# Prompt attention values taken head by head, with the high and low parts of values and of probabilities side by side

## What is computed

```python
    logits = jnp.einsum('bthd,btkhd->bhtk', q, k_sel).astype(jnp.float32) * (HEAD_DIM ** -0.5)
    logits = jnp.where(valid[:, None], logits, NEG)
    p = jax.nn.softmax(logits, axis=-1).astype(v_sel.dtype)
    return jnp.einsum('bhtk,btkhd->bthd', p, v_sel)
```

## Time and profile before

| what | value |
|---|---|
| median of 3 runs | 2734.62 us (2734.62 to 2734.95) |
| span of the profiled execution, first to last instruction | 2732.7 us |
| PE busy | 2707.3 us (99%), 18804 matmuls |
| DVE busy | 1729.2 us (63%) |
| ACT busy | 1103.5 us (40%) |
| POOL busy | 999.8 us (37%) |
| granted TensorE clock | 0.998 |

### The profile page before, as it was taken

How to read it: one execution, slowest core, us unless ns; L and a number is a source line. 1 busy time by engine, 2 the same in 40 slices (tenths; PEclk the granted TensorE clock), 3 DMA queues, 4 the chain that set the end, 5 groups by cost and what they waited for, 6 DMA issues and landing times. The chain is left out here.

```text
span 2732.7 us, 46951 instructions
## 1 busy us (share of the span) xinstructions
PE 2707.3 (99%) x18804; PEld 2646.4 (97%) x18804; DVE 1729.2 (63%) x2801; ACT 1103.5 (40%) x1858; POOL 999.8 (37%) x610
## 2 busy tenths in 40 slices
PE   9999999999999999999999999999999999999998
PEld 8999999998999999999999999999989999999997
DVE  8747576887433693838685647668773347837475
ACT  5324244636322352424443333454463224424242
POOL 2333333345433333333333333333544333333332
PEclk9999999999999999999999999999999999999999
DMA  3222222233122222222222222222332222222222
GB/s 118 99 71 93 77 87 93 88 124 125 63 71 91 75 73 84 78 93 78 94 77 85 70 95 78 92 86 88 132 109 70 77 88 74 75 79 78 93 78 85
DMA packets 72853, 238.04 MB, mean 87 GB/s; under 512 B 8304, under 2 KB 17264, under 8 KB 72176
## 3 DMA queue, kind: packets, MB, share of 16 engines
q1 hardware_dynamic: 57888, 208.30, 22.1%
q10 hardware_dynamic: 14800, 27.51, 2.9%
HBM read 227.52 MB, written 8.27 MB: 86 GB/s over the span
## 5 line engine op out<-in xcount | busy, mean ns | idle before, releaser
L498 POOL TENSOR_TENSOR w_lo<-w_raw,w_hi 128x1024 fp32r<-128x1024 f32 (+1 forms) x254 | 600.0, 2365 | 962.8 <-ACT w_hi L1131 947.7
L1131 ACT ACTIVATE w_hi<-w_raw 128x1024 fp32r<-128x1024 f32 (+1 forms) x238 | 250.2, 1051 | 796.1 <-PE lin L635 660.8
L635 PE MATMUL lin<-h_hi,w_hi 128*128 128x320 f32 x1600 | 373.8, 315 | 2.9 <-DVE tmp L1614 2.7
L635 PE MATMUL lin<-h_hi,w_lo 128*128 128x320 f32 x1600 | 364.6, 309 | 0.0
L635 PE MATMUL lin<-h_lo,w_hi 128*128 128x320 f32 x1600 | 364.1, 309 | 0.0
L635 PE MATMUL lin<-g_hi,w_lo 128*128 128x320 f32 x1408 | 320.9, 309 | 0.0
L635 PE MATMUL lin<-g_lo,w_hi 128*128 128x320 f32 x1408 | 320.8, 309 | 0.0
L635 PE MATMUL lin<-g_hi,w_hi 128*128 128x320 f32 x1408 | 320.7, 309 | 0.0
L550 POOL TENSOR_TENSOR lo_A<-raw_even,hi_A 128x512 fp32r<-128x512 f32 x120 | 167.8, 1398 | 376.3 <-ACT hi_A L1185 376.3
L635 PEld LDWEIGHTS lin<-h_hi,w_hi 128*128 128x128 f32 x1600 | 265.2, 188 | 15.9 <-issue 11.3
L635 PEld LDWEIGHTS lin<-h_lo,w_hi 128*128 128x128 f32 x1600 | 267.5, 188 | 0.0
(11 more groups left out here) (334 smaller groups left out, 6215.6 us busy)
## 6 DMA issues: line engine op xcount, KB each, us to landing
w_raw<-wts SPq DMA_DIRECT2D x240, 512.0 KB, 3.5
raw_even<-wts SPq DMA_DIRECT2D x88, 512.0 KB, 4.4
raw_odd<-wts SPq DMA_DIRECT2D x64, 512.0 KB, 4.2
caches<-kcache_in ACTq DMA_DIRECT2D x16, 512.0 KB, 4.0
caches<-vcache_in ACTq DMA_DIRECT2D x16, 512.0 KB, 4.7
x<-x_in SPq DMA_DIRECT2D x8, 320.0 KB, 6.6
k_out<-kT ACTq DMA_DIRECT2D x2, 1280.0 KB, 4.6
v_out<-v_sb ACTq DMA_DIRECT2D x2, 1280.0 KB, 8.6
```

The lines of the kernel that those rows point to most:

```text
L498: ins = nc.gpsimd.tensor_tensor(w_lo[:, s, cols], w_raw[:, s, cols], w_hi[:, s, cols].bitcast(F), ALU.subtract)
L635: ins = nc.tensor.matmul(out[:, half, :], w, a[:, half * HALF:(half + 1) * HALF], start=first and n == 0, stop=last and n == 2)
L1131: nc.scalar.activation(w_hi[:, s, 0:cols], w_raw[:, s, 0:cols], ACT.Copy).then_inc(hi_ready.sem, 1)
```

## The change

The weight block of the value product now holds one head: 64 columns of high and 64 columns of low values, side by side (hi, lo for head 0; lo, hi for head 1, so that the high rows land on the same 64 partitions as before). The moving operand is 256 columns of one head's probabilities: 128 high, 128 low. One pass of nb matmuls per head gives all four products, in 256 columns of PSUM of its own. ScalarE copies the lo x hi block across to the other 64 partitions (`keep_cross`, new, at step u+4 before `take_turned`), and VectorE adds hi x hi, hi x lo and lo x hi in four `tensor_tensor` instructions in place of two copies. The values' parts get buffers of their own, and splitting them takes two instructions of half the size on ScalarE and on VectorE. Before the last `conv_hi` ScalarE now waits for the last value product.

```diff
@@ weigh (PE)
-                    for i in range(3):
-                        if i == 2:
+                    for par in range(2):
+                        if par == 0:
+                            pe.wait_ge(pT_split.sem, pT_split.count(L, PROMPT_BEFORE[u]))
+                        else:
                             pe.wait_ge(pT_split.sem, pT_split.count(L, PROMPT_BEFORE[u] + 1))
                         for b in range(nb):
-                            v = v_lo[:, b, pair * P:(pair + 1) * P] if i == 0 else v_hi[pair % 2][:, b, :]
-                            ins = nc.tensor.matmul(out[:, 0:2 * P], v,
-                                                   pT[a][:, b, i // 2, :, :].rearrange("p two q -> p (two q)"),
-                                                   start=b == i == 0, stop=b == nb - 1 and i == 2)
+                            v = v_parts[pair % 2][b // 2][:, b % 2, 2 * par:2 * par + 2, :]
+                            ins = nc.tensor.matmul(out[:, par * 2 * P:(par + 1) * 2 * P],
+                                                   v.rearrange("p two d -> p (two d)"),
+                                                   pT[a][:, b, par, :, :].rearrange("p two q -> p (two q)"),
+                                                   start=b == 0, stop=b == nb - 1)
                 ins.then_inc(pv_done.sem, 1)
@@ split_v and keep_cross (ACT)
-                nc.scalar.activation(v_hi[pair % 2][:, :, :], v_sb[:, 0:4, pair * P:(pair + 1) * P],
-                                     ACT.Copy).then_inc(v_hi_done.sem, 1)
+                for half in range(2):
+                    ins = nc.scalar.activation(v_parts[pair % 2][half][:, :, 0:4:3, :], v_blocks(pair, half), ACT.Copy)
+                ins.then_inc(v_hi_done.sem, 1)
+
+            def keep_cross(L, u):
+
+                _, a, h = ATT_UNITS[u]
+                k = PROMPT_BEFORE[u] // 2
+                act.wait_ge(pv_done.sem, pv_done.count(L, ITEM_OF[u] + 1))
+                if k >= 2:
+                    act.wait_ge(o_halved.sem, o_halved.count(L, k - 1))
+                for par in range(2):
+                    to, from_ = slice(64 * par, 64 * par + 64), slice(64 - 64 * par, 128 - 64 * par)
+                    ins = nc.scalar.activation(cross[to, k % 2, :],
+                                               out_banks[ITEM_OF[u] % 2][from_, par * 2 * P:par * 2 * P + P], ACT.Copy)
+                ins.then_inc(cross_kept.sem, 1)
@@ the step loop (ACT), ahead of take_turned(L, step - 2)
+                    if 0 <= step - 4 < NU and ATT_UNITS[step - 4][0] == "prompt" and step - 4 == ITEMS[ITEM_OF[step - 4]][-1]:
+                        keep_cross(L, step - 4)
@@ behind the loop (ACT)
                 split(L, GATE_AT + 2)
+                act.wait_ge(pv_done.sem, pv_done.count(L, NI))
                 conv_hi(CB - 1)
@@ keep_out (DVE)
-                    dve.wait_ge(pv_done.sem, pv_done.count(L, ITEM_OF[u] + 1))
+                    k = PROMPT_BEFORE[u] // 2
+                    dve.wait_ge(cross_kept.sem, cross_kept.count(L, k + 1))
                     for par, lane in enumerate(lanes):
-                        ins = nc.vector.tensor_copy(qT[lane, h // 2, a * P:(a + 1) * P],
-                                                    out[lane, par * P:(par + 1) * P])
+                        ins = nc.vector.tensor_tensor(qT[lane, h // 2, a * P:(a + 1) * P], cross[lane, k % 2, :],
+                                                      out[lane, par * 2 * P:par * 2 * P + P], ALU.add)
+                    ins.then_inc(o_halved.sem, 1)
+                    dve.wait_ge(o_halved.sem, o_halved.count(L, k + 1))
+                    for par, lane in enumerate(lanes):
+                        o = qT[lane, h // 2, a * P:(a + 1) * P]
+                        ins = nc.vector.tensor_tensor(o, o, out[lane, par * 2 * P + P:(par + 1) * 2 * P], ALU.add)
                 ins.then_inc(o_kept.sem, 1)
@@ lo_v (DVE)
-                nc.vector.tensor_tensor(v_lo[:, 0:4, cols], v_sb[:, 0:4, cols], v_hi[pair % 2][:, :, :].bitcast(F),
-                                        ALU.subtract).then_inc(v_split.sem, 1)
+                for half in range(2):
+                    parts_ = v_parts[pair % 2][half]
+                    ins = nc.vector.tensor_tensor(parts_[:, :, 1:3, :], v_blocks(pair, half),
+                                                  parts_[:, :, 0:4:3, :].bitcast(F), ALU.subtract)
+                ins.then_inc(v_split.sem, 1)
```

More of the change, by code:

```diff
@@ L169, in build @@
         k_lo = at("k_lo", [P, AB, T], R, mix_at + 4 * part)
-        v_lo = at("v_lo", [P, TT, ATT_W], R, mix_at + 11 * part)
-        v_hi = [at(f"v_hi{i}", [P, 4, P], R, mix_at + 8 * part + 2048 * i) for i in range(2)]
+        v_parts = [[at(f"v_parts{i}_{h}", [P, 2, 4, HD], R, a) for h, a in enumerate(homes_)]
+                   for i, homes_ in enumerate(((mix_at + 8 * part, mix_at + 8 * part + 2048),
+                                               (g_hi_at + 4 * T * (KB - 1), g_lo_at + 4 * T * (KB - 1))))]
         masks = at("masks", [P, 10 * P], B16, mix_at + 15 * part)
@@ L183, in build @@
         o_rows = at("o_rows", [P, P], F, sq_at + 4 * 2 * P)
+        cross = at("cross", [P, 2, P], F, sq_at + 4 * 3 * P)
+        assert 4 * 5 * P <= 4 * T
         cache_words = AB * KEYS + 2 * ATT_W
@@ L269, in build, with v_blocks @@
         spread_out = bank[:, 0:4, 0:PART]
+        def v_blocks(pair, half):
+            return v_sb[:, 2 * half:2 * half + 2, pair * P:(pair + 1) * P].rearrange("p b (par d) -> p b par d", par=2)
         def res(slot):
@@ L373, in build @@
         v_split = Signal("v_split", PAIRS)
+        cross_kept = Signal("cross_kept", 4 * PAIRS)
+        o_halved = Signal("o_halved", 4 * PAIRS)
         pT_hi = Signal("pT_hi", NU)
@@ L1379, in take_turned @@
                         act.wait_ge(pv_done.sem, pv_done.count(L, item - 2))
-                    to = pT[a][:, 0:nb, 0, h % 2, :]
+                    to = pT[a][:, 0:nb, h % 2, 0, :]
                     src = src.rearrange("p (c q) -> p c q", q=P)
@@ L2092, in pT_lo @@
                 dve.wait_ge(pT_hi.sem, pT_hi.count(L, u + 1))
-                nc.vector.tensor_tensor(pT[a][:, 0:nb, 1, h % 2, :],
+                nc.vector.tensor_tensor(pT[a][:, 0:nb, h % 2, 1, :],
                                         turn_banks[u % 2][:, 0:nb * P].rearrange("p (c q) -> p c q", q=P),
-                                        pT[a][:, 0:nb, 0, h % 2, :].bitcast(F), ALU.subtract).then_inc(pT_split.sem, 1)
+                                        pT[a][:, 0:nb, h % 2, 0, :].bitcast(F), ALU.subtract).then_inc(pT_split.sem, 1)
             def lo_k(L, pair):
@@ L2109, in lo_v @@
             def lo_v(L, pair):
-                cols = slice(pair * P, (pair + 1) * P)
                 dve.wait_ge(v_hi_done.sem, v_hi_done.count(L, pair + 1))
-                nc.vector.tensor_tensor(v_lo[:, 0:4, cols], v_sb[:, 0:4, cols], v_hi[pair % 2][:, :, :].bitcast(F),
-                                        ALU.subtract).then_inc(v_split.sem, 1)
+                for half in range(2):
[3 more added lines that the diff above has]
+                ins.then_inc(v_split.sem, 1)
             nc.vector.memset(ones[:, :], 1.0).then_inc(evacuated.sem, 1)
```

## The result

| what | before | after |
|---|---|---|
| median, 4 runs each on one chip | 2734.78 us (2734.62 to 2735.14) | 2754.80 us (2754.17 to 2755.51) |
| span of the profiled execution | 2732.7 us | 2753.6 us |
| ratio | | 1.0073, 95% interval 1.0061 to 1.0085 |

The kernel became 20.0 us slower. The prediction had 8.4. The direction, the chain and most of its terms hold; the size does not.

A forecast was written before the change was run, and what follows sets the result against it. It took a VectorE-ScalarE chain as long as TensorE's to bound seven `logits` per layer: 5.13 us lateness less 0.95 us matmuls kept, 4.18 per layer, +8.4 us, giving 2743.0 us; range 2735 to 2748.

The forecast's parts named there:

- the seven places: Per layer, `logits` 8, 13, 18, 23, 28, 33, 38 wait for VectorE's maximum; slack 0.45 us at 18, 0.74 at 33.
- TensorE sets the pace: Rival: TensorE bounds the attention stage, so all saved matmuls count, -9.5 us: 2725.1 us; chance 0.08.
- VectorE, +0.64: `keep_out`: four additions one after the other take 1.25 us in place of 0.61, 0.64 us more.
- that rival (2739.2): Rival: `keep_out`'s additions overlap and add only 0.37 us, +4.6 us in all; chance 0.14.
- ScalarE, +0.57 where nothing is idle: `keep_cross` ahead of `take_turned`: 0.57 us late at steps 16, 26, 31, 0.13 at step 6, nothing at 11, 21, 36.
- Matmuls, 0.95 us per layer kept: `weigh`: only nb=1 and nb=2 savings count, 1.43 us per layer, less 0.48 passed by: 0.95 us.
- Costed at nothing: Low-part wait, `keep_out` of steps 8 and 13 (modulo 10), values' split, `conv_hi` wait, `keep_cross(4)`: no time added.
- more falls on the path: Rival: the kept 0.95 us are lost too, or the split values are not covered: 2745 to 2748 us; chance 0.11.
- (1): Sign in `weigh`: 160 matmuls where there were 240 in both layers, about 0.12 us apart.
- (2): Sign in `keep_out`: four additions from first start to next `invert` about 1.25 us; near 1.0 means overlap.
- (3): Sign on TensorE: idle time before `logits`, released by the maximum, goes from about nought to 14 us.
- (4): Sign on ScalarE: at steps 16, 26 and 31 `take_turned` starts some 0.57 us later after its step's `place_q`.

The follow-up runs named there:

- b_adds_on: Kernel before, with four additions replacing `keep_out`'s two copies only in steps 1 and 6 (modulo 10), ahead of a maximum that logits wait for: 2742.13 us, 1.0028.
- b_160: Kernel before without the pass of low values by high probabilities, so 160 prompt value matmuls in place of 240: 2730.16 us, 0.9984.
- a_240: Changed kernel with the second head's pass issued twice, so 240 value matmuls again with the same result: 2753.93 us.
- b_adds_off: Kernel before, with four additions replacing `keep_out`'s two copies only in steps 3 and 8 (modulo 10): 2736.56 us, 1.0008.
- a_own: Changed kernel with the 128x128 mask addition to the streams' own scores moved ahead of the third query rotation on VectorE: 2752.88 us, 1.0065.
- a_moved: Changed kernel with `keep_out` one step later on VectorE, right behind `row_max`: 2734.54 us, 0.9999.
- a_best: Changed kernel with `keep_cross` behind `exps`, `keep_out` behind `row_max`, the streams' rows' transpose behind the convolution blocks, the mask addition early: 2730.20 us, 0.9985.
- a_xmoved: Changed kernel with `keep_cross` alone moved behind `take_turned` and `exps` of its step on ScalarE: 2764.62 us, 1.0109.
- b_ kernels: Variants of the kernel before the change with something added, left out or moved: 2730.16 us to 2751.00 us.
- a_both: Changed kernel with `keep_cross` moved behind `exps` and `keep_out` behind the next `row_max`: 2735.13 us, 1.0002.

## Why the prediction was right in direction and wrong in size

By its own steps:

- **What bounds the kernel.** Right. At the seven places, five tight and two with slack, b_adds_on shows the forecast terms to 0.05 us each. What the reading missed is that at the two with slack TensorE set the pace (b_160). The rival that TensorE sets the pace (2725.1) falls with b_160, -4.3 and not -9.5, and with a_240.
- **VectorE, +0.64.** Measured 0.61. The additions do not overlap, so that rival (2739.2) falls. The rule on partition groups from the Trainium skill, "VectorE: DVE Perf Modes", section "Two Vector instructions with no wait between them", agrees with the trace here: 0.57 and 0.58 us for two pairs of some 0.28.
- **ScalarE, +0.57 where nothing is idle.** Right in place at 8, 18, 28 and 33, though the copies cost 0.68 us in the full queue of step 18. Wrong at 21: 0.50 us from the `keep_cross` of step 18, taken as covered.
- **Matmuls, 0.95 us per layer kept.** Failed: up to logits 38 nothing is kept (a_240). Even the nb=1 and nb=2 savings only lengthen the next wait, as at logits 11 and 13. The likely reason, argued and not tested: with waits at all seven places the delays on VectorE and ScalarE run from one place to the next without passing through `weigh`, and the prediction let the chain start anew behind TensorE too often.
- **"Costed at nothing".** This is the step that failed most. The `keep_out` of steps 8 and 13 (modulo 10) "stand before a row_max that no logits waits for at once", which is true; but ScalarE's `exps` waits for that maximum, its DMA issues, `conv_hi` and `take_turned` stand behind it, and VectorE's `pT_lo` behind those. The same idle time of ScalarE was also taken as cover for `keep_cross`. It cost about 1.0 us per layer by itself (b_adds_off), and with `keep_cross` of step 18 and what the parts do to each other some 2.3.
- **Sum per layer.** 4.18 predicted and 7.27 measured in layer 0: 0.95 of savings lost, 1.03 of additions off the path, 0.50 at logits 21, and some 0.6 left, most of it the parts together.
- **Outside the stages, taken as unchanged.** The end of each stage: TensorE's wait for the last convolution result, 0.74 us before and 1.52 after (1.33 already in b_adds_on), costs 0.4. The addition held up beside GpSimd in layer 1, and the rotations behind it: 2.0 (a_own). The clock, below: some 3.0 in the profiled execution.

In spans, +20.9 against +8.4: of the 12.5 us missed the stages are 6.4 (3.1 and 3.3), their ends 0.8, the way between them 2.0, the clock 3.0, and 0.3 the start less what the end takes back.

What it named as signs: (1) holds: starts in `weigh` are 0.12 us apart, except 0.19 to 0.20 behind the first matmul of each of the two accumulations, where the three passes before had one such gap, so that this `weigh` saves 0.42 us and not 0.48; (2) 1.22; (3) 14.4 us where 14 were forecast, a hit that says nothing of the size: a wait at these places does not show how much later than before the place itself was reached; (4) holds; (5) holds as it is worded, for the feed-forward blocks; what changed outside the stages, the projections of layer 1's mixer, no sign named. Of the rivals the one named "more falls on the path" went the right way, with an end, 2748, that was too near.

## What to carry to other kernels

When an engine works strictly in order, an instruction added off the critical path is not free until you have followed who waits for it next, and what stands behind that waiter, DMA issues among it; idle time can be spent as cover only once. Do the same work in another place before giving it up: moving `keep_out` behind the maximum gave back the whole 20 us, and only then were the saved matmuls worth anything (some 2.5 us). To see what a saving is worth, put the work back into the changed kernel and read the stage that it stands in: if that is no longer, the saving had been bought for nothing.

## What the runs showed of the hardware

**VectorE behind GpSimd.** A 0.22 us addition with both inputs in SBUF took 2.37 us when it started 0.20 us after a 2.42 us GpSimd instruction: it ended only 0.15 us after that had ended (rows above, and a_own). The Trainium skill, "SBUF — State Buffer", section "SBUF: two separate sides", says that the shared port pair is an exclusive lock for the whole instruction, taken by whoever starts first; the trace agrees, and shows that 0.2 us of alignment decide 2 us. The recorded starts don't tell exactly who was first: in layer 0 the same addition starts 0.05 us behind GpSimd's instruction in the kernel before and takes 0.22 us all the same, while GpSimd's takes 2.54 us instead of 2.42. In both layers of the changed kernel halves of the value split met GpSimd as well: at 2036.64 the pair takes 2.00 us, at 628.46 undisturbed 0.75.

**TensorE's clock.** In the profile after, the granted clock fell twice behind waits of TensorE. Windows of it, in layer 1 (busy times of PE, PEld, DVE, ACT, POOL, then the granted clock, DMA share, GB/s):

```profile
2034.00:2035.00 1.00, 0.52 (x4) 0.53 (x4) 0.74 (x2) 1.00 (x5) 0.00 (x0) 1.00 0.00 0
...
2036.00:2037.00 1.00, 0.22 (x2) 0.22 (x4) 0.94 (x6) 0.24 (x1) 0.67 (x2) 1.00 0.06 16
2037.00:2038.00 1.00, 1.00 (x7) 0.56 (x6) 1.00 (x2) 0.90 (x4) 1.00 (x1) 0.60 0.00 0
2038.00:2039.00 1.00, 1.00 (x5) 1.00 (x5) 1.00 (x4) 0.00 (x0) 0.57 (x2) 0.50 0.00 0
...
2040.00:2041.00 1.00, 1.00 (x25) 0.83 (x24) 0.41 (x2) 0.82 (x3) 0.91 (x1) 0.69 0.97 377
```

TensorE had waited 0.79 us for ScalarE and 1.03 us for the maximum within 3 us; then the granted clock was 0.50, which is 1.2 GHz, until 2040.6. Between logits 28 and 31 the kernel falls back 1.26 us, where in layer 0 it makes up 0.24: 1.5 us. A second such stretch follows the 1.51 us wait at 2077.39: from there to the product of the gate it takes 16.27 us instead of 14.74. In their profiles a_moved, a_own and a_best have one or two such stretches as well, behind the same wait of 1.5 us for the convolution result, and a_xmoved has two elsewhere in the stages. The b_ kernels and a_240, where that wait is at most 1.3 us, have none in the mixer, and neither has the profile of a_both, although it waits 1.52 us there twice. But a profile is one execution, and the clock of the others shows that the same kernel has such stretches in some executions and not in others: a_moved took 2732.7 to 2733.4 us in its four runs with a mean granted clock of 0.998 and 2734.4 to 2736.2 in its seven with 0.997, and a_both has 0.997 in four of its eleven. So the waits go with it and don't decide it alone; what does is left open, and medians of these kernels that differ by 1 to 3 us can differ by the clock alone.
